# Two-layer hybrid decoder trunk on one core: layer 0's in-projection for head h+1 run between the row blocks of attention head h

## What is computed

```python
proj = h @ w_in                                     # 1024 x 3072
# 4 differential heads: q, k of 2 x 64, v of 128 (causal, ALiBi)
p = softmax(s);  w = p[:, :, 0] - lam * p[:, :, 1];  o = rmsnorm(w @ v, subln_g) * (1 - lam_init)
# 8 dilated heads of 64 (three dilated windows, merged), run here as 4 pairs
y = concat([ya, yb]) @ w_out
```

## Time and profile before

| | us |
|---|---|
| median of 3 runs | 3126.89 (3126.61 to 3127.37) |
| the profiled execution | 3126.78 |
| its span, first to last instruction | 3125.0 |
| TensorE matmul busy | 2719.6 (87%) |
| VectorE busy | 1335.3 (43%) |
| ScalarE busy | 1115.5 (36%) |
| GpSimd busy | 1099.7 (35%) |
| mean granted clock of TensorE | 0.933 |

### The profile page before, as it was taken

How to read it: one execution, slowest core, us unless ns; L and a number is a source line. 1 busy time by engine, 2 the same in 40 slices (tenths; PEclk the granted TensorE clock), 3 DMA queues, 4 the chain that set the end, 5 groups by cost and what they waited for, 6 DMA issues and landing times.

```text
span 3125.0 us, 36011 instructions
## 1 busy us (share of the span) xinstructions
PE 2719.6 (87%) x12370; PEld 2230.4 (71%) x12370; DVE 1335.3 (43%) x1455; ACT 1115.5 (36%) x1650; POOL 1099.7 (35%) x458
## 2 busy tenths in 40 slices
PE   5999666778889999999998999665789999999996
PEld 3778555667667888778887778554667788788884
DVE  5644366454373015520257540567465104430045
ACT  2222256554333333333333222445333333322222
POOL 1434312120334444334443434212233444444442
PEclk8999787899989999999999999878899999999998
DMA  6657421210222223222324654211122232223222
GB/s 259 213 204 242 141 61 40 67 41 1 81 71 91 94 95 100 83 86 94 100 94 159 228 171 146 70 54 67 40 68 81 92 95 94 94 89 99 94 94 94
DMA packets 99598, 327.49 MB, mean 105 GB/s; under 512 B 11392, under 2 KB 11712, under 8 KB 99520
## 3 DMA queue, kind: packets, MB, share of 16 engines
q1 hardware_dynamic: 99520, 326.47, 32.4%
HBM read 297.07 MB, written 29.36 MB: 104 GB/s over the span
## 4 chain that ended last, share of the span: by engine, by line
issue 55%; PE 26%; POOL 12%; POOLq 3%; DVE 2%; DVEq 1%; ACT 1%; ACTq 0%
POOL w_lo L409 11%; PE ps L465 6%; PE ps L466 6%; PE ps L469 6%; PE ps L714 3%; PE ps L720 3%; PE ps L717 3%; POOLq L419 1%; POOLq L415 1%; POOL ybuf L432 1%; POOL arena L432 1%; DVEq L1133 0%; DVEq L1378 0%; DVE h_lo L1107 0%; ACT w_hi L768 0%
## 5 line engine op out<-in xcount | busy, mean ns | idle before, releaser
L409 POOL TENSOR_TENSOR w_lo<-w_raw,w_hi 128x1024 fp32r<-128x1024 f32 x394 | 965.8, 2454 | 1497.8 <-ACT w_hi L768 1497.7
L465 PE MATMUL ps<-h_hi,w_hi 128*128 128x512 f32 x2448 | 984.7, 402 | 104.0 <-ACT w_hi L768 65.0
L466 PE MATMUL ps<-h_lo,w_hi 128*128 128x512 f32 x2448 | 975.6, 399 | 0.0
L768 ACT ACTIVATE w_hi<-w_raw 128x1024 fp32r<-128x1024 f32 x394 | 414.6, 1057 | 728.7 <-PE ps L469 399.8
L465 PEld LDWEIGHTS ps<-h_hi,w_hi 128*128 128x128 f32 x2448 | 472.7, 193 | 233.2 <-issue 93.6
L469 PE MATMUL ps<-h_hi,w_lo 128*128 128x512 f32 x2448 | 607.0, 390 | 0.0
L466 PEld LDWEIGHTS ps<-h_lo,w_hi 128*128 128x128 f32 x2448 | 474.0, 194 | 97.8 <-issue 0.5
L469 PEld LDWEIGHTS ps<-h_hi,w_lo 128*128 128x128 f32 x2448 | 461.7, 189 | 96.6
L1474 DVE TENSOR_TENSOR arena<-arena,ps 128x512 f32 (+1 forms) x88 | 60.5, 687 | 783.7 <-PE ps L469 783.7
L1489 DVE TENSOR_TENSOR a_lo<-arena,a_hi 128x512 fp32r<-128x512 f32 x88 | 211.6, 2404 | 212.9 <-ACT a_hi L1063 212.5
L714 PE MATMUL ps<-a_hi,w_hi 128*128 128x512 f32 x704 | 174.4, 390 | 6.6 <-ACT a_hi L1063 6.6
(11 more groups left out here) (176 smaller groups left out, 2568.8 us busy)
## 6 DMA issues: line engine op xcount, KB each, us to landing
w_raw<-weights SPq DMA_DIRECT2D x394, 512.0 KB, 3.5
arena<-ada_w SPq DMA_DIRECT2D x80, 512.0 KB, 5.3
proj<-arena SPq DMA_DIRECT2D x48, 512.0 KB, 3.4
arena<-proj SPq DMA_DIRECT2D x64, 256.0 KB, 5.8
arena<-ada_w SPq DMA_DIRECT2D x4, 2048.0 KB, 19.7
arena<-proj SPq DMA_DIRECT2D x16, 512.0 KB, 3.7
arena<-proj SPq DMA_DIRECT2D x8, 1024.0 KB, 4.8
x<-xT SPq DMA_DIRECT2D x2, 2048.0 KB, 16.5
```

What stands on the lines that cost most here:

```text
L409: pool.tensor_tensor(w_lo[:, s, :], w_raw[:, s, :], w_hi[:, s, :].bitcast(f32), ALU.subtract).then_inc(lo_done, 1)
L465: pe.matmul(bank(b), w, h_hi[:, k, :], start=k == 0, stop=False)
L466: pe.matmul(bank(b), w, h_lo[:, k, :], start=False, stop=False)
L768: a.activation(w_hi[:, slot, :], w_raw[:, slot, :], ACT.Copy).then_inc(hi_done, 1)
```

## The change

`project` is gone for layer 0, and so is its store to and load from DRAM. Both halves of h are split ahead of time (`hh`, `hl`, the second pair in the arena), for which the statistics of x half 1 are taken at the start and x half 1 is loaded ahead of the adaLN weights. A unit is loaded and cast once and used for both halves. The unit of work on TensorE is a *chunk*: one unit for one half. The six chunks of head 0 (q, k and v for two halves) run before the attention, those of head b+1 in row blocks 0 to 5 of head b, each first in its row block. Their results go from PSUM straight to the split q, k (slot b % 2) and to `v_sb`.

```diff
+        def chunk_of(c):
+            if c < 6:
+                return ((0, 0), (1, 0), (0, 1), (1, 1), (2, 0), (2, 1))[c]
+            return c // 2, c % 2
+        def chunk_bank(c):
+            return 7 if c >= 6 or c % 2 == 0 else 6
...
+            def chunk(c):
+                u, half = chunk_of(c)
+                if c > 1:
+                    before = c - 2 if c < 7 else c - 1
+                    if before % 6 < 4:
+                        pe.wait_ge(qk_lo, qk_count(before))
+                    else:
+                        pe.wait_ge(v_out, v_count(before))
+                unit(u, u % 2, chunk_bank(c), half if c in (0, 2) else None, hh[half], hl[half], done=ch_done)
...
                 for n in range(8):
+                    if n < 6 and not last:
+                        chunk(6 * (b + 1) + n)
+                        if (b, n) == (6, 5):
+                            pe.drain().then_inc(unit_used, 24)
                     if kind == 1:
                         turn_weights(n)
```

ScalarE reads a chunk out (`evict`: the high part of q or k, or v), VectorE takes the low part of q or k from the same bank. The casts of weights (`hi_u`) stand in ScalarE's iterations 3, 5 and 7:

```diff
                         if n < 7:
                             exps(n + 1)
-                        if n < 5:
-                            split(b + 1, 1 - slot, n - 1, last)
+                        if n < 7 and not last:
+                            evict(6 * (b + 1) + n - 1)
+                        if n == 3 and not last:
+                            hi_u(3 * b + 5)
+                        if n in (5, 7) and b < 6:
+                            hi_u(3 * b + 6 + n // 6)
...
+                        if 0 < n < 5 and not last:
+                            evict(6 * (b + 1) + n - 1)
+                        if b < 6:
+                            ada_step(8 * b + n)
```

The scores no longer stack q's parts on the partitions. They are three products over 64 rows for each map, the two maps in turn:

```diff
-                        for part in (k_high, k_low):
+                    for term, (q, k) in enumerate(((q_high, k_high), (q_low, k_high), (q_high, k_low))):
+                        for c in range(2):
+                            rows = slice(64 * c, 64 * c + 64)
                             mm = pe.matmul(ps[:, c * 1024 + k0:c * 1024 + k0 + w],
-                                           q_split[slot][:, c, n * P:(n + 1) * P], part[slot][:, c, k0:k0 + w],
+                                           q[slot][rows, n * P:(n + 1) * P], k[slot][rows, k0:k0 + w],
```

```diff
+                sp.wait_ge(pv_done, 8 * HEADS + 1)
+                for half in range(2):
+                    t = slice(half * HALF, (half + 1) * HALF)
+                    sp.dma_start(x[:, :, t], x_in[:, :, t]).then_inc(x_again, 16)
```

At the start VectorE takes both reciprocals of the norm behind its sums, before it hands them over:

```diff
                     v.drain()
+                inverse(0, 0, g)
+            v.drain().then_inc(acc_done, 1)
             columns(0, 0, 2)
```

More of the change, by code:

```diff
@@ L103, in trunk_kernel @@
         ada_acc = arena[:, 3072:6144].rearrange("p (g n) -> p g n", g=3)
[L106 to L112, removed]
@@ L314, in body @@
                     for s in range(2):
[L315 to L317 removed]
+                        unit(PACK_IN[1] + 2 * i + s, use + 2 * i + s, (use + s) % 2)
                     if ada:
@@ L456, in _, with unit @@
             pe.sem_inc(pv_done, 1)
-            def unit(use, s, b, job=None):
+            def unit(use, s, b, job=None, high=h_hi, low=h_lo, y_new=False, done=unit_used):
                 pe.wait_ge(hi_done, use + 1)
@@ L733, in _ @@
             mean(0, 0, 0)
+            mean(0, 0, 1)
             ada_turn(0, 2, acc_first)
             for layer in range(2):
-                for half in range(2):
-                    use = in_base(layer, half)
-                    pairs(layer, "in", half, use, T_IN[layer] + PAIRS_IN * half, PAIRS_IN, h_job(layer, 0, half))
-                    if layer == 1:
+                if layer == 0:
+                    attention()
+                else:
+                    for half in range(2):
+                        use = in_base(1, half)
+                        pairs(1, "in", half, use, T_IN[1] + PAIRS_IN * half, PAIRS_IN, h_job(1, 0, half))
                         if half:
@@ L1105, in h_low @@
                 v.wait_ge(hh_done, 8 * h_job(layer, kind, half) + k + 1)
+                dst, high = (hl[half], hh[half]) if (layer, kind) == (0, 0) else (h_lo, h_hi)
                 if kind == 1:
@@ L1438, in _ @@
                     v.drain()
+                inverse(0, 0, g)
+            v.drain().then_inc(acc_done, 1)
             columns(0, 0, 2)
-            for k in range(KB + 1):
-                if k < KB:
-                    xn(0, 0, 0, k)
-                if k:
-                    h_low(0, 0, 0, k - 1)
+            for half in range(2):
+                for k in range(KB + 1):
+                    if k < KB:
+                        xn(0, 0, half, k)
+                    if k:
+                        h_low(0, 0, half, k - 1)
+                    if half and k in (6, 8):
+                        evict((k - 6) // 2)
+            evict(2)
+            evict(3)
             for layer in range(2):
-                project(layer, 0)
-                low(layer, 0, 1)
-                project(layer, 1)
                 if layer == 0:
```

480 lines of the change are left out of this document (280 added, 200 removed).

## The result

The changed kernel takes **3266.68 us** (median of 4 runs, 3264.68 to 3269.36), the one before beside it 3126.75 (4 runs): a ratio of **1.0449**, 95% interval 1.0431 to 1.0468. It is 4.5% slower. The prediction was 3232, with the range from 3140 to 3310 and 0.86 on slower.

A forecast was written before the change was run, and what follows sets the result against it. No engine was taken to bound attention, but a chain of short steps across TensorE, VectorE and ScalarE. Start -267.7, heads +386.1 and the rest -13.3 gave net +105 on 3126.89: 3232 us, range 3140 to 3310.

The forecast's parts named there:

- the ring: Row blocks: unit, scores, turn, bias, exponentials, two evictions run one after another before the next unit; TensorE idles 4.4 to 5.7 us.
- Rival (4): Heads: the bank wait isn't last, a row block costs TensorE's work alone; 2968 us, chance 0.11 with its halfway case.
- A heads: The four differential heads carrying units: 90.2 us plus 12 of clock each, 408.8 us together.
- B heads: The three dilated heads carrying units, twice the transposes: 101.6 us plus 12 of clock each, 340.8 us together.
- everything behind: After the heads: out-projection with h already split and second half's first unit start sooner, -13.3 us; from the FFN on unchanged.
- half of such a spell is lost: Units in heads: dense work behind idle gaps starts at half clock, losing 1.45 to 2.95 us; 2.0 taken, 84 us.
- Rivals (1) and (3): Heads: the clock holds, 3148 us, chance 0.12; or stays low for whole units, 3376 us, chance 0.04.
- "the rest" of a head: From row block 7's bias to the next head's second score: 20.6 us in A, 23.4 in B, plus 0.5.
- a round: One pass from unit to unit in a head, five behind the opening: 62.1 us together in A, 70.6 in B.
- The low end: Scores in heads: the two members of a pair share one 0.227 us slot, three slots per 512 columns.
- rival (2): Scores in heads don't pair, each matmul takes its own slot: +54 us, 3286 us, chance 0.13.
- Rival (5): Heads: a late transfer or weight cast adds 1 us of wait in a row block: +42, 3274 us, chance 0.05.

The follow-up runs named there:

- Runs 1 to 3: Changed kernel with the unit last in its row block (2992.68 us), both evictions queued earlier (3072.69 us), or ScalarE's eviction alone queued earlier (3165.40 us).
- run 1: Changed kernel with the unit moved from first to last place of its row block on TensorE: 2992.68 us, 0.9577 of the kernel before.
- run 6: Changed kernel plus 32 unused matmuls behind row blocks 0 and 1 of heads 0 to 6: 3236.23 us.
- run 8: Changed kernel with both maps' scores reading the same 64 rows: 3319.03 us.
- run 9: Changed kernel with the 16 one-column adaLN matmuls moved from head end to the end of the next head's row block 0, VectorE's part also later: 3265.13 us.
- run 10: run 1's order with the 16 one-column adaLN matmuls moved into the next head's row block 0, ahead of its unit, VectorE's part also later: 3016.11 us.
- run 2: Changed kernel, unit still first, both evictions queued ahead of the next row block's exponentials and bias: 3072.69 us, 0.9839 of the kernel before.
- run 4: Changed kernel with the unit between scores and transposes (A heads: scores, unit, turn, weigh; B heads: turn, weigh, unit, scores): 3175.97 us.
- run 7: Changed kernel with the six score matmuls of a tile ordered map by map: 3265.20 us.

## Why the prediction was right, and where it was 35 us short

**The mechanism was right.** Idle time before the stalled units is 4.1 to 5.6 us (forecast 4.4 to 5.7), released by VectorE's eviction or, for the first v unit, by ScalarE's; the eviction stands right behind the exponentials; all of these units but the first one begin at half clock (that one, at 120.69 us, begins at full clock and loses it within its first two matmuls); the heads' clock is 0.81. Runs 1 to 3 show that the place of the unit and that of its evictions make the ring: opening it from TensorE's side gives back 274 us, from the evictions' side 194. Rival (4), the other side, put 2968 us on a kernel in which a row block costs TensorE's work alone. The changed kernel isn't that, but run 1 is, with 2993 us: A heads of 68.3 us (66 in the rival's sum) and B heads of 78 to 79 (74).

**The terms**, in the profiled executions (spans 3262.9 and 3125.0, difference +137.9):

| | forecast | measured |
|---|---|---|
| start, to the second score of head 0 | -267.7 | -264.3 |
| four A heads | 408.8 | 420.2 |
| three B heads | 340.8 | 357.1 |
| last head, to its last transpose | 45.4 | 47.7 |
| heads against 408.9 before | +386.1 | +416.1 |
| everything behind | -13.3 | -13.9 |
| net | +105 | +137.9 |

(The last head ends at 886.46 + 47.7 = 934.2; what stands behind is the difference of the spans less the other two.)

*Start.* The first unit began at 65.6 us instead of 61.6; the rest followed as forecast.

*Clock.* Forecast 42 x 2.0 = 84 us. Measured against the 5.65 us of a unit at full clock (run 6), the 42 units lost 322.7 - 42 x 5.65 = 85.4 us. The step from the earlier trace rows, "half of such a spell is lost", held in size, and run 6 shows the cause for the units behind gaps. But the prediction took 2.0 us for all 42, and the first unit of each head has no gap in front: the 35 behind gaps lost 73.4 us, and six of the other seven 12.0 all the same, for which no cause is shown. That the total came so near is in part luck. Rivals (1) and (3), with none or all of a unit cold, fall.

*What was mis-sized* lies around the unit and the scores. A unit at full clock takes 5.65 us to the next instruction, not the 5.44 that the earlier trace rows gave between unit and unit: 42 x 0.21 = 8.8 us. A tile's scores take 0.23 us more than their slots: three slots of 0.227 for 512 columns are 0.68, and 0.90 was measured; 1.25 and 1.59 for 768 and 1024 columns, against 1.02 and 1.36. Six of these a head, in seven heads, are 9.7 us. The sum also has 5.1 us for five scores whose 24 slots make 5.44: 0.34 x 7 = 2.4 us. And "the rest" of a head is not what it was: from the bias of row block 7 to the next head's second score head 1 takes 22.6 us and head 5 25.2, where 21.1 and 23.9 were forecast; 1.4 x 7 = 9.8 us. In A heads 1.0 of it was a choice of row: the kernel before took 21.6 us in its first two heads, and the prediction's 20.6 is the third's. With the clock's 1.4 these make 32.1 us, where the seven heads were 27.7 us short (the last head's 2.3 come on top), so the other terms of a round came out some 4 us shorter together. The idle time before a unit begins at 4.1 us, for one, where 4.4 was the least forecast.

The first two of these have two parts, which run 1 tells apart. The last eight matmuls of two of its units at full clock, and what follows: scores over 64 rows (head 0), and transposes over 128 (head 4).

```profile
147.02 1.98 PE L507 MATMUL ps<-h_hi,w_lo 128*128 128x512 f32 x8
148.93 1.66 PE L604 MATMUL ps<-qk_flat 64*128 64x512 f32 x12
```

```profile
396.31 1.98 PE L507 MATMUL ps<-h_hi,w_lo 128*128 128x512 f32 x8
398.13 0.82 PE L625 MATMUL ps<-ident,pr_flat 128*128 128x128 f32 x6
```

From start to start the first takes 1.91 us, 0.09 more than eight slots of 0.227, and the second 1.82, no more than the slots. The same 0.09 us stand behind the scores, where TensorE goes back to 128 rows (their last pair of 512 columns takes 0.32 us to the next instruction). The Trainium skill (TensorEngine Tiling (Array Packing), Key Properties) says that a change of tiling mode drains TensorE; these rows agree, though they don't tell a drain from another cost of the change. The prediction named this and counted nothing for it. The other part, 0.08 to 0.11 us at the first matmul of a unit, is no change of rows: it is there too behind weighing over 128 rows (143.27 to 143.58 in run 1, for a slot of 0.227). The first pair of a tile of scores has it too. What causes it stays open.

*Scores.* The low end was right: run 8 prices the other case at +52 us, near the +54 of rival (2). Rival (5), a late transfer: in the seven heads no unit's first matmul waits for a cast, a low part or a transfer.

*Handover.* The prediction doesn't name the 16 matmuls of the adaLN column at the end of a head and so counts nothing for them; run 9 shows that in the changed kernel they cost nothing, since VectorE's bias step ends last there, and run 10 what they cost where no gap takes them in.

## What to carry to other kernels

In this kernel independent work put into the gaps of a serial chain filled them only if it was placed behind the step that feeds the chain, or, for most of the gain, if what frees its own buffer wasn't queued behind that chain on another engine. Follow every way round, not only the one over the data: buffers that are handed back (here the probabilities, over the transposes) and in-order queues (ScalarE's output ahead of its exponentials) closed rings of their own here. The same instructions in another order went from 4.5% slower to 4.2% faster than before.

## What the runs showed of the hardware that I had not expected

- Useless matmuls pay when they stand in front of dense work: 448 of them, in idle time of 4.1 to 5.0 us, took 30 us off (run 6).
- A gap's length alone doesn't tell the clock. In run 2 units behind 1.3 to 2.2 us of idle time mostly took 5.7 us; in run 4, behind 1.0 to 1.8 us, they took between 5.6 and 8.4, and the same unit of different heads differed by as much. The clock can also fall inside a unit that has begun at full speed. Run 4, matmuls 0.23 us apart, and 0.43 from 249.3 on:

```profile
248.66 0.39 PE L504 MATMUL ps<-h_lo,w_hi 128*128 128x512 f32 x1
248.88 0.39 PE L503 MATMUL ps<-h_hi,w_hi 128*128 128x512 f32 x1
249.11 0.41 PE L504 MATMUL ps<-h_lo,w_hi 128*128 128x512 f32 x1
249.34 0.61 PE L503 MATMUL ps<-h_hi,w_hi 128*128 128x512 f32 x1
249.74 0.63 PE L504 MATMUL ps<-h_lo,w_hi 128*128 128x512 f32 x1
```

- Score matmuls over 64 rows start in pairs whichever way the program orders the two maps (run 7), as long as their rows differ (run 8).
